# A reordered opening: conditioning loaded and turned alone, its Silu ahead of the rows' norm, a modulation chunk ahead of the turns

## The chip, the cores and the metric

The kernel runs on one core of a Trainium2 chip (trn2). The metric is the device time of one execution in microseconds. The same program is run several times and the median counts. Beside the times stands one profiled execution, whose span (first to last instruction) is a little different from the median; prices are read from it.

## What is computed

Two layers of a hybrid trunk over two tiles of 128 tokens (a context prompt and a latent sample), width 1024. Each layer has a mixer and a mixture of 32 experts. Every norm is modulated by a linear function of a conditioning vector, one for each tile:

```python
mod = jax.nn.silu(cvec) @ w_mod[l] + b_mod[l]
sh1, sc1, g1, sh2, sc2, g2 = jnp.split(mod[:, None, :], N_MOD, axis=-1)
h = rms_norm(x, norm_mix[l]) * (1.0 + sc1) + sh1
# layer 0: h -> differential attention and gated DeltaNet; layer 1: h -> gated spatial mixing
x = x + g1 * out
h = rms_norm(x, norm_ffn[l]) * (1.0 + sc2) + sh2
x = x + g2 * hier_moe(h, ...)
```

`cvec` is `c_ctx` for the context tile and `c` for the latent tile. All is float32. The weights of one layer's modulation are 1024 x 6144, and nearly all of the kernel's 288 MB read from HBM are weights.

## The kernel before

The program is written by hand, engine by engine, with semaphores. `P` is 128, `KT` is 8 (blocks of the width), `NB` is 2 (tiles). Activations are kept turned: `xT` and `hT` hold features on partitions and tokens in the free dimension.

**Weights.** SyncE's queue issues all weight loads in the order of a list, `loads`, written out by hand. A piece of 2 MB (a "chunk": 1024 rows by 512 columns) goes as two loads of 1 MB into one of four ring slots or six further slots, and its slot must have been freed (semaphore `used`, raised by TensorE's last matmul on the piece). The list begins with the modulation chunks (0,0) and (0,2), then the lower halves of two pieces of `w_in_even`, then chunks (0,1) and (0,3). Ahead of them the queue loads the identity and the ones, `const[:, 0:2P]` (line 802).

**ScalarE's queue** issues 12 loads before any arithmetic (lines 1585 to 1596): the rows of the two tiles (`xin`), the conditioning vectors `c_ctx` and `c` (16 rows of `vec1`), the constants up to `C_LEV` (which hold triangles, rotation tables, routing tables and, near the end, epsilon), and then bias, norm weights, convolution weights and two small vectors into `vec1` and `vec2`.

**The opening on TensorE** (lines 832 to 903), in order: wait for all ten small loads (`ld_vec`) and turn `vec1` and `vec2` into bank 0; wait for `xin` and the constants; turn the normalised rows `xn` of tile 0, then of tile 1, 8 blocks of 128x128 each (`rows_in`, line 842); clear bank 7 with a matmul of zeros; wait for `condT`; modulation chunks (0,0) and (0,2), 64 matmuls each (`mod_chunk`, line 861); turn the raw rows of tile 0; turn the modulation's result (`mod_turn`, line 870); and so on to the first projection (`first_rows`, line 908).

**The opening on VectorE** (lines 2014 to 2025): wait for the turned vectors and copy them to `cols` (bias, norm weights, conditioning and convolution taps, one column each); then wait for the scales and scale tile 0's rows into `xn`; then copy the turned rows out of PSUM.

**The opening on ScalarE** (lines 1640 to 1653): load the table of logarithm and exponential, wait for `xin` and the constants, two squares with a sum along the row, logarithm and exponential (`inv_root`), which give the scales `xsum`; scale tile 1's rows; load the Silu table; wait for `cols`, and take the Silu of the conditioning's 16 columns into `condT`.

Later, at line 1670, ScalarE's queue loads the rest of the constants, and behind it eleven small loads, with the gate weights `wab` first.

Of the kernel before, what the change touches and what calls it, by code (L numbers as in the profile page):

```python
# [24 lines left out]
P = 128  # L25
# [66 lines left out]
C_ID, C_ONE, C_TRI = 0, P, 2 * P  # L92
# [10 lines left out]
C_EPS = C_COL + 3  # L103
C_LEV = C_EPS + 2
# [8 lines left out]
V_COND = V_NMIX + DEPTH * KT  # L113
V_NFFN = V_COND + NB * KT
# [52 lines left out]
class Semaphores:  # L167
# [3 lines left out]
    def __init__(self, sem):  # L171
        self.a_ab = sem("a_ab")
# [37 lines left out]
        self.ld_attn = sem("ld_attn")  # L210
        self.ld_const = sem("ld_const")
# [19 lines left out]
        self.t_at = sem("t_at")  # L231
        self.t_cy = sem("t_cy")
# [34 lines left out]
        self.v_abx = sem("v_abx")  # L267
# [10 lines left out]
        self.v_gll = sem("v_gll")  # L278
# [40 lines left out]
def build(nc, I, O):  # L319
    ctx = ExitStack()  # L320
    with ctx:
# [43 lines left out]
        def part(at, shape):  # L365
            n = int(np.prod(shape))
            v = scratch[:, at:at + n]
            if len(shape) == 2:
                v = v.rearrange("p (a b) -> p a b", b=shape[1])
            elif len(shape) == 3:  # L370
                v = v.rearrange("p (a b c) -> p a b c", b=shape[1], c=shape[2])
            elif len(shape) == 4:
                v = v.rearrange("p (a b c d) -> p a b c d", b=shape[1], c=shape[2], d=shape[3])
            return v
# [17 lines left out]
        xin = part(2 * P, (NB, D))  # L392

# [266 lines left out]
        def _(sp):  # L660
# [141 lines left out]
            sp.dma_start(const[:, 0:2 * P], I["consts"][:, 0:2 * P]).then_inc(S.ld_vec, 16)  # L802
# [22 lines left out]
        def _(pe):  # L825
# [6 lines left out]
            pe.wait_ge(S.ld_vec, 16 * 10)  # L832
            nc.tensor.transpose(bank[0][:, 0:P], vec1[:, :], ident)
            nc.tensor.transpose(bank[0][:, P:P + 86], vec2[0:86, :], const[0:86, C_ID:C_ID + 86]).then_inc(S.t_x, 1)
            pe.wait_ge(S.ld_x, 32)
            pe.wait_ge(S.ld_const, 16)
# [8 lines left out]

            pe.wait_ge(S.v_xt, 1)
            rows_in(xn, 0, (1, 2))
            pe.wait_ge(S.a_xt, 1)
            rows_in(xn, 1, (3, 4))
# [47 lines left out]
            mod_chunk(0, 0)  # L897
            mod_chunk(0, 2)
# [88 lines left out]
            pe.wait_ge(S.v_ab, 1)  # L987
            for g in range(4):
                last = mm(bank[6][:, g * H:(g + 1) * H], tri[g % 2], gdec[:, g * H:(g + 1) * H], start=True, stop=True)
# [584 lines left out]
        def _(act):  # L1574
# [9 lines left out]

            act.dma_start(xin[:, 0, :], I["x_prompt"][0]).then_inc(S.ld_x, 16)
            act.dma_start(xin[:, 1, :], I["x_sample"][0]).then_inc(S.ld_x, 16)
            act.dma_start(vec1[112:120, :], I["c_ctx"].rearrange("(m p) -> m p", p=P)).then_inc(S.ld_vec, 16)
            act.dma_start(vec1[120:128, :], I["c"][0].rearrange("(m p) -> m p", p=P)).then_inc(S.ld_vec, 16)
            act.dma_start(const[:, 2 * P:C_LEV], I["consts"][:, 2 * P:C_LEV]).then_inc(S.ld_const, 16)
# [49 lines left out]

            roots()  # L1640
            act.wait_ge(S.ld_x, 32)
            act.wait_ge(S.ld_const, 16)
# [9 lines left out]
            act.wait_ge(S.v_cols, 1)  # L1652
            A(condT[:, :, :].rearrange("p t k -> p (t k)"), cols[:, V_COND:V_COND + NB * KT], ACT.Silu).then_inc(S.a_silu_c, 1)
# [16 lines left out]
            act.dma_start(const[:, C_LEV:NC_COLS], I["consts"][:, C_LEV:NC_COLS]).then_inc(S.ld_const, 16)  # L1670
# [76 lines left out]
            act.wait_ge(S.v_abx, 1)  # L1747
# [5 lines left out]
            A(t16a, t16a, ACT.Ln, bias=onec).then_inc(S.a_ab, 1)  # L1753
# [33 lines left out]
            act.wait_ge(S.v_gll, 1)  # L1787
# [191 lines left out]
        @block.gpsimd  # L1979
        def _(pool):  # L1980
            pool.memset(zeros[:, :], 0.0).then_inc(S.g_set, 1)

            pool.memset(raw[:, :, :, 0:2].rearrange("p c t n -> p (c t) n"), 0.0)
            pool.memset(raw[:, :, :, P + 2:P + 4].rearrange("p c t n -> p (c t) n"), 0.0).then_inc(S.g_set, 1)
            pool.wait_ge(S.ld_const, 32)
            for lev in range(1, NLEV + 1):
                for t in range(NB):
                    if lev == 1:
                        pool.wait_ge(S.v_att, 2 * t + 2)
                    else:  # L1990
                        pool.wait_ge(S.t_lx, 2 * lev - 3 + t)
                    nc.gpsimd.tensor_tensor(blk_B[t], blk_L[t], level(FIRST - 1 + lev), ALU.mult).then_inc(S.g_bm, 1)

            for t in range(NB):
                pool.wait_ge(S.a_y1, t + 1)
                pool.wait_ge(S.g_bm, 2 * NLEV)
                for d in range(2):
                    g, r = 2 * t + d, slice(d * HB, d * HB + HB)
                    nc.gpsimd.tensor_tensor(heads(g_V[g][r, :]), heads(y1s[t][r, :]),
                                            beta[r, g * H:(g + 1) * H].unsqueeze(2).to_broadcast([HB, H, P]), ALU.mult).then_inc(S.g_v1, 1)  # L2000
# [3 lines left out]
        def _(dve):  # L2004
# [123 lines left out]
            V.tensor_reduce(lame, lamq.rearrange("p (a n) -> p a n", a=2), AX.X, ALU.add).then_inc(S.v_abx, 1)  # L2128
            convolve(2)
            dve.wait_ge(S.a_ab, 1)  # L2130
# [10 lines left out]
            dve.wait_ge(S.ld_const, 32)  # L2141
# [56 lines left out]
            def delta_rows(t):  # L2198
# [27 lines left out]
                if t == 0:  # L2226
                    V.tensor_tensor(ekd, gll[:, 0:8], gcc[:, 0:8], ALU.subtract).then_inc(S.v_gll, 1)
# [448 lines left out]
```

## Time and profile before

| | before |
|---|---|
| median of 3 executions | 857.33 us |
| lowest to highest | 852.7 to 859.1 us |
| span of the profiled execution | 856.0 us |
| TensorE busy | 787.9 us, 92% |
| mean DMA throughput | 340 GB/s, 291.47 MB |
| mean granted TensorE clock | 0.971 |

The profiled execution lies 1.3 us under the median and well inside the spread of the three. All instants below are microseconds from the start of the span. TensorE's busy time includes waits inside its pipeline and is no measure of its peak.

### The profile page before, as it was taken

Reading aid. Unit: us, or ns where it says so; the run is one execution under the profiler, and the core shown is the slowest. Engines: PE = TensorE matmul, PEld = TensorE weight load, DVE = VectorE, ACT = ScalarE, POOL = GpSimd, SP = SyncE. Lnnn points to the kernel's source line nnn. Section 1 sums busy time; section 2 is a strip of 40 time slices with the busy share of each in tenths; the row PEclk is TensorE's granted clock in tenths of the full one; section 3 lists DMA queues with packets and bytes.
Section 4 is the critical chain, followed back from the end, with each engine's and each line's share of the span. In section 5 each row is a group of like instructions: output and inputs, shape, how many; then the busy total and the mean of one; then the engine's idle time right before and its main releaser. Section 6 shows DMA issues by size and latency. Waiting matters only on the chain.

```text
span 856.0 us, 15977 instructions
## 1 busy us (share of the span) xinstructions
PE 787.9 (92%) x6913; PEld 524.1 (61%) x6913; DVE 321.9 (38%) x687; ACT 166.7 (19%) x323; POOL 12.7 (1%) x17
## 2 busy tenths in 40 slices
PE   4999999998999999999787889989999999978797
PEld 3788577677898655565444344889865465534344
DVE  1154467653415434333413240241534433440224
ACT  3112321322204111111110141211311111110012
POOL 0000001020000000000000000000000000000000
PEclk9998999999999999999989999999999999997898
DMA  9999579496997799999999999994579999999991
GB/s 343 387 347 334 197 248 354 148 346 211 293 410 272 281 384 361 387 416 416 418 415 411 399 384 386 392 399 141 197 306 363 357 377 417 415 419 416 410 396 66
DMA packets 97879, 291.47 MB, mean 340 GB/s; under 512 B 11833, under 2 KB 14991, under 8 KB 87567
## 3 DMA queue, kind: packets, MB, share of 16 engines
q1 hardware_dynamic: 86960, 284.32, 86.5%
q10 hardware_dynamic: 10847, 6.11, 2.4%
q8 instruction: 56, 0.92, 0.4%
q14 instruction: 16, 0.13, 0.0%
HBM read 288.30 MB, written 2.10 MB: 339 GB/s over the span
## 4 chain that ended last, share of the span: by engine, by line
PE 72%; DMA 11%; SPq 8%; DVE 3%; ACT 2%; issue 2%; ACTq 1%; DVEq 0%
PE psum L1358 7%; PE psum L1265 7%; PE psum L1344 6%; PE psum L1334 6%; PE psum L908 6%; DMA scratch<-in_w_exp_up 6%; PE psum L1390 5%; PE psum L968 5%; SPq L745 5%; PE psum L861 4%; DMA ring<-in_w_exp_up 4%; PE psum L1401 3%; PE psum L1516 3%; PE psum L1529 3%; PE psum L1030 2%
## 5 line engine op out<-in xcount | busy, mean ns | idle before, releaser
L1344 PE MATMUL psum<-scratch,hT 128*32 128x512 f32 (+1 forms) x352 | 79.2, 666 | 17.6 <-DMA scratch<-in_w_exp_up 17.6
L1334 PE MATMUL psum<-scratch 128*128 128x128 f32 x704 | 82.4, 275 | 1.0 <-DVE scratch L2461 1.0
L1334 PEld LDWEIGHTS psum<-scratch 128*128 128x128 f32 x704 | 80.3, 192 | 1.3 <-issue 1.3
L1344 PE MATMUL psum<-ring,hT 128*32 128x512 f32 x320 | 60.1, 630 | 10.7 <-DMA scratch<-in_w_exp_up 10.7
L908 PE MATMUL psum<-hT,ring 128*128 128x256 f32 x256 | 57.8, 382 | 1.1 <-DVE hT L2052 0.7
L1401 PEld LDWEIGHTS psum<-const,scratch 128*128 128x128 bf16 x480 | 45.1, 97 | 21.4 <-issue 13.6
L1265 PE MATMUL psum<-hT,ring 128*128 128x128 f32 x512 | 58.0, 275 | 0.0
L1265 PEld LDWEIGHTS psum<-hT,ring 128*128 128x128 f32 x512 | 57.7, 192 | 0.5 <-issue 0.5
L1401 PE MATMUL psum<-const,scratch 128*128 128x256 bf16 x480 | 55.9, 272 | 1.5 <-DVE scratch L2477 1.5
L2470 DVE TENSOR_SCALAR hT<-psum,const 128x512 f32<-128x512 f32 x22 | 16.5, 751 | 106.3 <-PE psum L1390 93.6
L908 PEld LDWEIGHTS psum<-hT,ring 128*128 128x128 f32 x256 | 47.8, 190 | 9.6 <-DVE hT L2052 2.0
L1358 PE MATMUL psum<-scratch,hT 128*64 128x512 f32 (+1 forms) x256 | 50.0, 594 | 2.4 <-DMA ring<-in_w_exp_up 2.4
L1886 ACT ACTIVATE scratch<-psum 128x256 f32<-128x256 f32 x22 | 8.4, 383 | 221.3 <-PE psum L1344 133.6
L1390 PE MATMUL psum<-scratch,const 128*32 128x512 f32 (+2 forms) x336 | 50.9, 596 | 0.0
L1344 PEld LDWEIGHTS psum<-ring,hT 128*32 128x32 f32 x320 | 15.6, 115 | 53.4 <-issue 53.4
L1344 PEld LDWEIGHTS psum<-scratch,hT 128*32 128x32 f32 (+1 forms) x352 | 22.4, 128 | 39.7 <-issue 39.7
L861 PE MATMUL psum<-ring,condT 128*2 128x128 f32 x1344 | 43.4, 285 | 1.7 <-issue 1.0
L2481 DVE TENSOR_TENSOR scratch<-psum,scratch 128x256 f32<-128x256 f32 x22 | 9.3, 425 | 94.2 <-ACT scratch L1886 94.1
L968 PE MATMUL psum<-ring,hT 128*128 128x512 f32 x96 | 42.6, 597 | 0.0
L861 PEld LDWEIGHTS psum<-ring,condT 128*2 128x2 f32 x1344 | 34.6, 88 | 9.0 <-issue 4.7
L1358 PEld LDWEIGHTS psum<-scratch,hT 128*64 128x64 f32 (+1 forms) x256 | 15.3, 127 | 33.3 <-issue 33.2
L968 PEld LDWEIGHTS psum<-ring,hT 128*128 128x128 f32 x96 | 17.8, 190 | 20.8 <-issue 20.8
(328 smaller groups left out, 977.0 us busy)
## 6 DMA issues: line engine op xcount, KB each, us to landing
ring<-in_w_mod SPq DMA_DIRECT2D x42, 1024.0 KB, 9.5
scratch<-in_w_exp_down SPq DMA_DIRECT2D x36, 1024.0 KB, 18.1
scratch<-in_w_exp_gate SPq DMA_DIRECT2D x22, 1024.0 KB, 18.3
scratch<-in_w_exp_up SPq DMA_DIRECT2D x22, 1024.0 KB, 18.5
ring<-in_w_exp_gate SPq DMA_DIRECT2D x18, 1024.0 KB, 16.5
ring<-in_w_exp_up SPq DMA_DIRECT2D x18, 1024.0 KB, 18.4
scratch<-in_w_exp_gate SPq DMA_DIRECT2D x32, 512.0 KB, 13.3
scratch<-in_w_exp_up SPq DMA_DIRECT2D x32, 512.0 KB, 13.9
```

Of the source, the lines that this page charges most:

```text
L745: sp.dma_start(slot(s)[:, at:at + 1024], w[e][:, 1024 * kh:1024 * kh + 1024]).then_inc(full[s], 16)
L861: last = mm(bank[mbank[g]][32 * m:32 * m + NB, at:at + P], condT[:, :, k], w[:, k, m * P:(m + 1) * P], start=(k == 0), stop=(k == KT - 1))
L908: last = mm(out[:, c2 * T:(c2 + 1) * T], w[:, k, m * P:(m + 1) * P], hT[:, k, :, :], start=(k == 0 and k1 == KT), stop=(k == k1 - 1), skip ...
L968: last = mm(bank[b], hT[:, k, t, :], w[:, k, :], start=(k == 0), stop=(k == KT - 1))
L1265: last = mm(bank[2 * t + m // 4][:, (m % 4) * P:(m % 4 + 1) * P], w[m // 4][:, k, (m % 4) * P:(m % 4 + 1) * P], hT[:, k, t, :], start=(k = ...
L1334: last = mm(bank[b][:, k * P:(k + 1) * P], hrow[:, t, half * 4 + k, :], Pm[:, t, :], start=(t == 0), stop=(t == 1))
L1344: last = mm(bank[0][i * m:(i + 1) * m, :], xg[:, k, i * m:(i + 1) * m], w[e][:, k, :, :], start=(k == 0), stop=(k == KT - 1))
L1358: last = mm(bank[0][i * m:(i + 1) * m, :], xg[:, 4 * kh + k, i * m:(i + 1) * m], w[i // 2][:, i % 2, k, :, :], start=(kh == 0 and k == 0), ...
L1390: last = mm(bank[1 + half][i * m:(i + 1) * m, :], hidT[:, a, i * m:(i + 1) * m], slot(slots[e // 2])[:, base:base + 512], start=(a == 0), ...
L1401: last = mm(bank[4 + k // 2][:, (k % 2) * T:(k % 2 + 1) * T], y3[:, j, k, :], ohT, start=False, stop=True, skip_group_check=True)
L1516: last = mm(bank[4 + 2 * j + t], hT[:, k, t, :], w[:, k, :], start=(k == 0), stop=(k == KT - 1))
L1529: last = mm(bank[b][:, (m % 2) * T:(m % 2 + 1) * T], w[:, k, m * P:(m + 1) * P], hT[:, k, :, :], start=(k == 0), stop=(k == KT - 1))
```

## The change

- The conditioning vectors get a buffer of their own (`cond_rows`) and are the first two loads on ScalarE's queue, ahead of the rows. With the first load of constants they count on a new semaphore, `ld_cond`.
- Epsilon moves next to identity and ones, so that the first load on SyncE's queue brings it. The load of the other constants at the start is gone; they come with the later load, which is now `C_TRI` to the end.
- TensorE first turns the 16 conditioning rows alone into bank 5. The turns of `vec1` (now 112 rows) and `vec2` become a function, `vector_columns`, which is called behind modulation chunk (0,0). The row turns stand behind that, and chunk (0,2) behind them.
- ScalarE loads the Silu table first, takes the Silu of the conditioning straight from PSUM, and then loads the other table and goes on with the rows' squares.
- Three semaphores are merged into others (`a_ab` into `a_e1`, `v_abx` into `v_ab`, `v_gll` into `v_att`), and waits on the constants are adapted to one load.

```diff
-C_ID, C_ONE, C_TRI = 0, P, 2 * P
+C_ID, C_ONE, C_EPS = 0, P, 2 * P
+C_TRI = C_EPS + 2
...
-C_EPS = C_COL + 3
-C_LEV = C_EPS + 2
+C_LEV = C_COL + 3
...
-V_COND = V_NMIX + DEPTH * KT
-V_NFFN = V_COND + NB * KT
+V_NFFN = V_NMIX + DEPTH * KT
...
+        cond_rows = part(2 * P + NB * D, (P,))
...
-            sp.dma_start(const[:, 0:2 * P], I["consts"][:, 0:2 * P]).then_inc(S.ld_vec, 16)
+            sp.dma_start(const[:, 0:C_TRI], I["consts"][:, 0:C_TRI]).then_inc(S.ld_cond, 16)
...
-            pe.wait_ge(S.ld_vec, 16 * 10)
-            nc.tensor.transpose(bank[0][:, 0:P], vec1[:, :], ident)
-            nc.tensor.transpose(bank[0][:, P:P + 86], vec2[0:86, :], const[0:86, C_ID:C_ID + 86]).then_inc(S.t_x, 1)
-            pe.wait_ge(S.ld_x, 32)
-            pe.wait_ge(S.ld_const, 16)
+            pe.wait_ge(S.ld_cond, 16 * 3)
+            nc.tensor.transpose(bank[5][:, 0:NB * KT], cond_rows[0:NB * KT, :], const[0:NB * KT, C_ID:C_ID + NB * KT]).then_inc(S.t_cond, 1)
+
+            def vector_columns():
+
+                pe.wait_ge(S.ld_vec, 16 * 7)
+                nc.tensor.transpose(bank[0][:, 0:V_NFFN], vec1[0:V_NFFN, :], const[0:V_NFFN, C_ID:C_ID + V_NFFN])
+                nc.tensor.transpose(bank[0][:, V_NFFN:NV], vec2[0:86, :], const[0:86, C_ID:C_ID + 86]).then_inc(S.t_x, 1)
...
-            pe.wait_ge(S.v_xt, 1)
-            rows_in(xn, 0, (1, 2))
-            pe.wait_ge(S.a_xt, 1)
-            rows_in(xn, 1, (3, 4))
...
             mod_chunk(0, 0)
+            vector_columns()
+            pe.wait_ge(S.v_xt, 1)
+            rows_in(xn, 0, (1, 2))
+            pe.wait_ge(S.a_xt, 1)
+            rows_in(xn, 1, (3, 4))
             mod_chunk(0, 2)
             pe.wait_ge(S.a_xt, 3)
             rows_in(xin, 0, (4, 5))
...
             pe.wait_ge(S.v_ab, 1)
+            pe.wait_ge(S.ld_const, 16)
             for g in range(4):
...
+            act.dma_start(cond_rows[0:KT, :], I["c_ctx"].rearrange("(m p) -> m p", p=P)).then_inc(S.ld_cond, 16)
+            act.dma_start(cond_rows[KT:2 * KT, :], I["c"][0].rearrange("(m p) -> m p", p=P)).then_inc(S.ld_cond, 16)
             act.dma_start(xin[:, 0, :], I["x_prompt"][0]).then_inc(S.ld_x, 16)
             act.dma_start(xin[:, 1, :], I["x_sample"][0]).then_inc(S.ld_x, 16)
-            act.dma_start(vec1[112:120, :], I["c_ctx"].rearrange("(m p) -> m p", p=P)).then_inc(S.ld_vec, 16)
-            act.dma_start(vec1[120:128, :], I["c"][0].rearrange("(m p) -> m p", p=P)).then_inc(S.ld_vec, 16)
-            act.dma_start(const[:, 2 * P:C_LEV], I["consts"][:, 2 * P:C_LEV]).then_inc(S.ld_const, 16)
...
+            gates()
+            act.wait_ge(S.t_cond, 1)
+            A(condT[:, :, :].rearrange("p t k -> p (t k)"), bank[5][:, 0:NB * KT], ACT.Silu).then_inc(S.a_silu_c, 1)
             roots()
             act.wait_ge(S.ld_x, 32)
-            act.wait_ge(S.ld_const, 16)
+            act.wait_ge(S.ld_cond, 16 * 3)
             for t in range(NB):
...
             gates()
-            act.wait_ge(S.v_cols, 1)
-            A(condT[:, :, :].rearrange("p t k -> p (t k)"), cols[:, V_COND:V_COND + NB * KT], ACT.Silu).then_inc(S.a_silu_c, 1)
...
-            act.dma_start(const[:, C_LEV:NC_COLS], I["consts"][:, C_LEV:NC_COLS]).then_inc(S.ld_const, 16)
+            act.dma_start(const[:, C_TRI:NC_COLS], I["consts"][:, C_TRI:NC_COLS]).then_inc(S.ld_const, 16)
...
-            act.wait_ge(S.v_gll, 1)
+            act.wait_ge(S.v_att, 4)
             A(ekd, ekd, ACT.Exp).then_inc(S.a_kd, 1)
```

## Rows read from the trace of the kernel before

**Rows 1.** The page's engine table: busy us, share of the span, instructions.
```profile
PE 787.9 (92%) x6913; PEld 524.1 (61%) x6913; DVE 321.9 (38%) x687; ACT 166.7 (19%) x323; POOL 12.7 (1%) x17
```

**Rows 2.** Chain of waits in order of time, opening: start us, us, what.
```profile
1.17 0.46 ACTq L1586
...
2.64 0.37 ACTq L1589
...
5.63 5.88 DMA scratch<-in_subln
...
11.55 0.47 PE psum L833
...
12.21 0.38 DVE cols L2015
12.59 0.67 DVE scratch L2017
...
13.40 3.65 PE psum L842 x16
...
17.59 4.08 PE psum L861 x128
21.66 1.02 PE psum L842 x8
```

**Rows 3.** Chain of waits, 44 to 69 us.
```profile
44.57 14.07 PE psum L908 x64
...
59.06 9.27 DMA ring<-in_w_mod
```

**Rows 4.** Stretches: length, busy PE, PEld, DVE, ACT, POOL, PEclk, DMA share, GB/s.
```profile
10.00:12.00 2.00, 0.45 (x2) 0.29 (x2) 0.00 (x0) 1.94 (x5) 0.00 (x0) 1.00 1.06 379
...
54.00:56.00 2.00, 2.00 (x11) 1.77 (x10) 2.00 (x6) 0.00 (x0) 0.00 (x0) 1.00 0.56 177
```

**Rows 5.** DMA issues: KB each, us from issue to landing.
```profile
scratch<-in_x_sample ACTq DMA_DIRECT2D x1, 512.0 KB, 6.4
...
const<-in_consts ACTq DMA_DIRECT2D x1, 308.5 KB, 6.7
...
const<-in_consts ACTq DMA_DIRECT2D x1, 416.0 KB, 6.9
```

**Rows 6.** Timeline of ScalarE, opening: start us, us, engine, line, operation.
```profile
5.98 1.28 ACT L1579 ACT_TABLE_LOAD   x1 [5.98 <-issue]
...
9.45 1.06 ACT L1646 ACTIVATE scratch<-scratch 128x1024 f32<-128x1024 f32 x1 [2.19 <-DMA const<-in_consts]
...
12.13 0.20 ACT L1603 ACTIVATE small<-small 128x2 f32<-128x2 f32 x1
```

**Rows 7.** View of line L699, one load: the second half of chunk (0,0).
```profile
L699 SPq DMA_DIRECT2D ring<-in_w_mod x1: 500/500/500, 1.6 to 1.6; - x1
DMA to landing us min/median/max: 11.2/11.2/11.2
```

**Rows 8.** TensorE: ns min/median/max, first to last start us; stretch as rows 4; timeline.
```profile
L842 PE MATMUL psum<-const,scratch x7: 421/421/421, 14.7 to 16.0; 128*128 128x128 f32 x7
...
L861 PE MATMUL psum<-ring,condT x12: 273/372/418, 18.1 to 18.6; 128*2 128x128 f32 x12
...
80.00:86.80 6.80, 6.80 (x76) 5.21 (x77) 4.99 (x18) 0.82 (x5) 0.00 (x0) 0.50 0.77 269
...
32.79 1.93 PE L861 MATMUL psum<-scratch,condT 128*2 128x128 f32 x64
...
81.53 3.60 PE L861 MATMUL psum<-ring,condT 128*2 128x128 f32 x64
```

**Rows 9.** Timeline and one line's view: first uses of what lands later.
```profile
77.24 4.35 PE L952 MATMUL psum<-wab,hT 128*128 128x16 f32 x32
...
99.35 1.22 DVE L2146 SCALAR_TENSOR_TENSOR scratch<-scratch 128x1024 f32<-128x1024 f32 x1
...
L1788 ACT ACTIVATE small<-small x1: 200/200/200, 166.7 to 166.7; 128x8 f32<-128x8 f32 x1
```

## What the change will do: the prediction

> **What bounds the kernel now.** I read the page's engine table first: over the profiled span (856.0 us, table of times) TensorE (PE) is busy 787.9 us, VectorE 321.9, ScalarE 166.7 [rows 1]. So the kernel advances with TensorE and the weight transfers that feed it. The edit is all in the first 23 us, so the chain of waits of the opening comes next [rows 2]. TensorE does nothing until the last small vector has landed at 11.51. It turns the vectors (11.55 to 12.21, 0.66), VectorE copies the columns (0.38) and scales the first tile's rows (0.67, from 12.59), TensorE turns 16 blocks of rows (from 13.40, 3.65), clears a bank (17.05 to 17.59, 0.54) and does two modulation chunks, 128 matmuls, in 4.08. At 21.66 it goes on to the next turns, `mod_turn(M_LO)` and the first projection. I take this instant, "the end of chunk (0,2)", as the yardstick: everything behind it is unchanged in order.
>
> Whether a shift of that instant reaches the end is seen further down the chain [rows 3]. From 44.57 TensorE works unbroken to 58.64. Then the weight queue, which waited for a slot to be freed by that work, issues a load that lands 9.27 us later, and TensorE waits for it until 68.37. Each load on this stretch starts when TensorE frees its slot, so a shift of TensorE shifts the load. The DMA engines have room there: between 54 and 56 us their busy share was 0.56, against 1.06 between 10 and 12 [rows 4]. So I let the shift pass to the end whole, in both directions; where it did not, the rival "absorbed" below stands.
>
> **What goes from the front of the chain.** The old first wait (11.51) is gone as a release of the conditioning: the two 4 KB vectors are now first on ScalarE's queue, and identity, ones and epsilon come in one load on SyncE's queue at 0.72. Their landing has no row. From below they need at least their issue (nothing, counted from the issue), from above 512 KB of x_sample on the same queue took 6.4 us [rows 5]. I take some 3 us from their issues, as they are small and first; even if they landed at 11 nothing would change, since the chunk's weights are later (next part). The small turn, the zero matmul (0.54 in the chain) and the Silu (0.21 us of ScalarE) then lie in time in which TensorE was idle. ScalarE pays one more table load, 1.28 us [rows 6]. Its first table load began at 5.98, behind 12 issues of 0.4 to 0.5 us each; one of these, that of the constants, is gone. It used to start the squares only at 9.45, on the constants' landing. Now it runs: issues to 5.98 - 5.98/12 = 5.5, 5.6 taken, Silu's table to 6.9, Silu to 7.1, the other table to 8.4. x_sample landed at 1.17 + 6.4 = 7.6 [rows 2, 5], and both x loads are issued two issues later, about 1 us, so at 8.6 at worst. From squares to the scales takes 9.45 to 12.33, 2.9 us [rows 6], so they are there by 11.5. By the next part they are wanted at 16.5, so the extra table load and the later x cost nothing unless they slip by five more microseconds.
>
> **What sets the new chain: the weights of chunk (0,0).** In the old order its landing was hidden. Its second half was issued at 1.6 and took 11.2 us, so 12.8 [rows 7]. The diff takes the 308.5 KB load of constants out of the early traffic. It had landed at 2.64 + 6.7 = 9.3 [rows 2, 5], ahead of that half, so its bytes come off whole: 0.316 MB at 379 GB/s [rows 4] is 0.8 us. I take 12.0. The bound above is 12.8 (no byte argument). Chunk (0,2) is the next 2.1 MB of the queue, 5.5 us at that rate: 17.5.
>
> Behind this wait, in TensorE's own order, now stand the vectors' turns, and behind them on VectorE the copy `cols`, and behind that, in VectorE's order, the scaling of tile 0's rows. The rows' scales are ready at 11.5, but VectorE meets the column copy first in its program and waits there. So the chain is: 12.0, chunk (0,0), vector turns 0.66, then from the column copy to the first row turn (12.21 to 13.40) 1.19 us, idle for TensorE, 16 row turns, chunk (0,2).
>
> **TensorE's clock decides the prices.** The 16 row turns of 13.40 follow each other every 228 ns, the 8 of 21.66 every 128 [rows 2]; one of the former takes 421 ns, and the chunk's matmul goes from 418 to 273 ns between 18.1 and 18.6 [rows 8]. In the stretch 80.0 to 86.8, where the granted clock is 0.50 (1.2 GHz), the 64 matmuls of a chunk took 3.60 us, against 1.93 at 32.79, at the granted 1.00 (2.4 GHz) [rows 8]. The view of the granted clock shows 1.00 for 0 to 18.5 too, but the durations say the half level. So the 16 row turns ran at half speed (3.65 us, where 8 at full clock took 1.02), and the clock was full from about 18.5, 5.1 us after the unbroken work had begun at 13.40. The edit moves a chunk of 64 matmuls into the slow time: 3.5 us from its start to the next work where the old place cost under 2.
>
> The sum, with the old distance of 5.1 us from the start of the work to the full clock taken over (12.0 + 5.1 = 17.1, an estimate): 12.0 + 3.5 + 0.66 + 1.19 = 17.35, then 16 turns at full clock 2.05, then the chunk 1.9: 21.3. Before: 21.66. The gain is 0.3 to 0.4 us. Bare counting of what left the chain would have promised 0.54 + 2.04 = 2.6. The Trainium skill ("TensorE: Matmul & The Clock Gate", part 1) says that the default state is throttled and activity releases the throttle; by that rule the earlier work also brings the full clock earlier, which is the case "clock early" below, with its own price. The same page of the Trainium skill ("Architectural detail", part 1) calls VectorE's queue strictly first in, first out. That speaks against this edit, since the scaling then cannot overtake the column copy; the trace agrees, with scales ready at 12.13 + 0.20 = 12.33 [rows 6] and the scaling on the chain only from 12.59, where the copy ends [rows 2]. If it could overtake, the row turns could follow the vectors' turns at 16.15 and the sum would be 20.1.
>
> **The rest of the diff.** The later load of constants grows from 416 to 724.5 KB and is still one issue at 42.8. The small one took 6.9 us [rows 5]; scaled by bytes, 12 us, it lands near 55. The first instruction behind a wait for it is VectorE's L2146 at 99.35; the gate weights queued behind it on ScalarE's queue are read at 77.24 [rows 9]. At least 19 us lie before each of them: nothing. If the cover were gone it would cost what the bytes cost, 0.8 us; the total of bytes is the same. Three semaphores are merged. `v_att` 4 in place of `v_gll` comes later on VectorE, but ScalarE reaches that exponential (L1788) only at 166.7, behind `first_inverse(0)`, which itself waits for work that VectorE does after the last `v_att` [rows 9]: nothing. Shorter turns and a copy of 198 instead of 214 columns: under 0.05 us.
>
> Sum: 856.0 - 0.3 = 855.7 for a profiled execution; against the median of 857.33, which lies 1.3 above it, 857.0.
>
> **Rivals.**
> Clock early: the clock is full before the chunk's end or from its start. From the start: 12.0 + 1.9 + 0.3 + 1.2 + 2.05 + 1.9 = 19.4, 2.2 us less than 21.66; near its end, 0.8 less. For it: TensorE starts 1.4 us earlier than 13.4 and does denser work than the broken start at 11.55. Against it: it is a cold start in both. Time 855.1 to 856.5.
> Clock late, the one on the other side: the idle 1.2 us between the vectors' turns and the row turns breaks the work, and the clock rises only 5.1 us after the row turns start, at 22.5. Then 17.4 + 3.65 = 21.05, 1.45 us of the chunk at half speed (0.41 of it), the rest 1.1: 23.6, 1.9 us later than before. It decides as soon as the clock is still at half when the first row is turned. For it: the old start too had a break (12.2 to 13.4) and the rise came only 5.1 us after the break. Time 859.2.
> Absorbed: the opening ends earlier but the transfers after it don't, so 857.3. For it: TensorE waited 0.8 us for a load at 68.4. Against it: that load starts with a slot that TensorE frees.
> Half-clock stretches fall elsewhere: there is one at 80 to 86.8 us, and every other stretch after it moves with the work. One more or less of that length costs 6.8 x 0.5 = 3.4 us; the three runs of before spread from 852.7 to 859.1, which such stretches may explain. Two or three of one sign would be needed to pass 1%.
>
> **Chances.** Forecast (-0.3) 0.40; clock early 0.22; clock late 0.25; absorbed 0.06; moved stretches that carry it beyond 1% 0.07, split 0.03 faster and 0.04 slower. The first four lie between 855.1 and 859.2. To them comes the spread of a median of few runs: the fastest run of before, 852.7, and the slowest, 859.1, which with the late clock's 1.9 is 861.0. So 852.5 to 861.0. About 1% is what a measurement of this kernel can tell from no change: faster 0.03, same 0.93, slower 0.04.
>
> **What would show it.** In the changed profile: the conditioning's turn near 4 to 5 us and its Silu by 7.2; ScalarE's squares starting at 8 to 9 and the scales by 11.6; TensorE idle until the landing of chunk (0,0) at about 12.0, 64 matmuls in about 3.5 us; the row scaling on VectorE right behind the column copy, near 16.6, and not at 11.5; the first row turn at 17.4; the end of chunk (0,2) at 21.3, and 228 or 128 ns from one row turn to the next to tell the clock cases. At 58 and 68 us the same shift should be seen. I am wrong if chunk (0,0) lands well before 11 (the order of the two queues matters more than bytes), if the scaling does not wait for the columns, or if a shift at 22 us is not there at 68 us.

## The result, and the profile after

The changed kernel takes 858.93 us in the median of 22 executions (854.95 to 864.2), the kernel before 856.06 us beside it, in as many (852.7 to 860.47). The ratio is 1.0027, 95% interval [1.0014, 1.004]: slower by 2.3 us (the two medians lie 2.9 apart). That is less than 1%, so inside what the prediction called the same, but it is a loss where a gain of 0.3 us was forecast. The changed kernel was timed against the one before twice more, on other occasions, with 12 executions of it each (runs `c1_changed_again` and `f2_changed_third`): 0.9998 [0.997, 1.0025] and 1.0009 [0.9983, 1.0034]. Weighting the three by the inverse square of their half-widths gives 1.0019 with a half-width of 0.0011, so some 1.7 us. Executions more than 1.5% above the fastest of their kernel are left out of all ratios here (one of `f1_cols_first_again` at 1021.46 us, two of `c4_warm12` at 867.89 and 868.09), though not out of the medians.

The engine table of the changed kernel's first profile has nearly the numbers of [rows 1]; this one execution (853.9 us of span) is even shorter than the one profiled before (856.0), though the medians stand the other way. A single profile can't carry a difference of 2 us here.

```profile
span 853.9 us, 15978 instructions
...
PE 787.4 (92%) x6914; PEld 523.3 (61%) x6914; DVE 321.7 (38%) x687; ACT 167.9 (20%) x324; POOL 12.7 (1%) x17
```

The chain of waits of that profile (start us, us, what) answers to [rows 2] and [rows 3]. Line 858 is the chunk's matmul, 844 the row turns, 837 the vectors' turns, 910 the projection:

```profile
1.65 10.60 DMA ring<-in_w_mod
...
12.38 3.48 PE psum L858 x64
15.87 0.25 PE psum L837
...
16.23 0.37 DVE cols L2018
16.59 0.67 DVE scratch L2020
...
17.31 1.97 PE psum L844 x16
19.27 1.86 PE psum L858 x64
21.13 1.02 PE psum L844 x8
...
58.53 9.76 DMA ring<-in_w_mod
...
68.33 1.93 PE psum L858 x64
```

The opening is the predicted chain almost to the tenth: the wait for the weights of chunk (0,0), the chunk at half clock in 3.5 us, the vectors' turns, the column copy and, behind it, the row scaling, the first row turn at 17.31 (forecast 17.4), the end of chunk (0,2) at 21.13 (forecast 21.3, before 21.66). The 0.53 us won are gone at 68.33, where the chain of before also stood (68.37). So this execution explains no loss. A second and a third profile of the same kernel (chain of waits again, first `c1_changed_again`) look otherwise:

```profile
12.30 3.59 PE psum L858 x64
...
17.53 3.50 PE psum L844 x16
21.04 1.86 PE psum L858 x64
22.90 1.03 PE psum L844 x8
...
60.31 9.86 DMA ring<-in_w_mod
```

and now `f2_changed_third`:

```profile
12.29 3.60 PE psum L858 x64
...
17.53 3.68 PE psum L844 x16
21.21 1.96 PE psum L858 x64
23.16 1.02 PE psum L844 x8
...
60.57 9.95 DMA ring<-in_w_mod
...
70.56 1.47 PE psum L858 x45
```

Up to 17.5 us all three agree within 0.25 us. Then the same 16 row turns take 1.97 us in the first and 3.50 and 3.68 in the others: full clock against half. Chunk (0,2) ends at 22.9 and 23.2, the delay reaches 70.2 and 70.6 where chunk (0,5) starts. This is the rival "clock late" (forecast 23.6). In this text "late branch" stands for these two openings.

What the opening does and what the whole execution takes are not tied closely. The spans of the three changed profiles are 853.9, 854.6 and 862.6 us, those of the three profiles of before 856.0, 853.9 and 857.1. The second changed profile is a late branch and still ends among the shortest. The chains show what the opening costs up to 70 us; that this makes the difference of the medians is an inference, supported by the timings below and not proved by any one profile.

### The profile page after: what moved, and what is told of

The parts are those of the page before. It is cut to its first block, busy times and chain, and to the rows that moved or that the text cites. A ratio compares the mean times of both kernels' runs of the same rounds, so it can differ in the third digit from the quotient of the medians.

```text
span 853.9 us, 15978 instructions
## 1 busy us (share of the span) xinstructions
PE 787.4 (92%) x6914; PEld 523.3 (61%) x6914; DVE 321.7 (38%) x687; ACT 167.9 (20%) x324; POOL 12.7 (1%) x17
## 4 chain that ended last, share of the span: by engine, by line
PE 74%; DMA 11%; SPq 6%; DVE 3%; ACT 2%; issue 2%; ACTq 1%; DVEq 0%
PE psum L1347 8%; PE psum L1361 7%; PE psum L1337 7%; PE psum L1268 7%; PE psum L910 6%; PE psum L1393 6%; DMA scratch<-in_w_exp_up 5%; PE psum L970 5%; PE psum L858 4%; PE psum L1404 4%; DMA ring<-in_w_exp_up 4%; PE psum L1519 3%; PE psum L1532 3%; SPq L744 3%; DMA ring<-in_w_mod 2%; PE psum L1033 2%
## 5 line engine op out<-in xcount | busy, mean ns | idle before, releaser
L1347 PE MATMUL psum<-ring,hT 128*32 128x512 f32 x320 | 60.1, 630 | 10.7 <-DMA scratch<-in_w_exp_up 10.7
## 6 DMA issues: line engine op xcount, KB each, us to landing
scratch<-in_w_exp_down SPq DMA_DIRECT2D x36, 1024.0 KB, 17.5
```

Of the source, the lines that this page charges most:

```text
L1347: last = mm(bank[0][i * m:(i + 1) * m, :], xg[:, k, i * m:(i + 1) * m], w[e][:, k, :, :], start=(k == 0), stop=(k == KT - 1))
```

## The experiments

In all of them "before" is the kernel before, run beside. The experiments came in five groups, each on one chip; ratios within a group share their "before". Two theories are tried. The theory "clock": the idle 1.2 us between the vectors' turns and the row turns lets the full clock come late in part of the executions. The theory "constants": the grown later load of constants holds up the weights issued at 51 us. These are two loads of 1 MB of `w_in_even`, on the same queue ahead of those for chunk (0,5); their landing below is that of the first.

**One part undone or moved.** `e1_const_back` restores the early load of the constants:

```diff
+            act.dma_start(const[:, C_TRI:C_LEV], I["consts"][:, C_TRI:C_LEV]).then_inc(S.ld_const, 16)
             act.dma_start(vec1[0:DEPTH * MT, :], ...)
...
-            act.dma_start(const[:, C_TRI:NC_COLS], ...)
+            act.dma_start(const[:, C_LEV:NC_COLS], ...)
```

> The changed kernel, with the constants loaded in two parts again as before (C_TRI to C_LEV early, behind the x loads; the rest at the later place). Theory 'constants': the later load, grown by 0.3 MB, holds up the weights queued at 51 us by up to 0.8 us, so this kernel is 0.6 to 0.8 us faster than the changed one, ratio to before 1.0017 to 1.002, and in its trace w_in_even's first half issued near 51 lands before 59.7 instead of 60.16. Theory 'clock': the loss is the row turns and chunk (0,2) done at half clock in some executions; then nothing changes, ratio 1.0027, the landing may move but the time does not.

Measured: 857.67 us, ratio 1.0005 [0.9991, 1.002]. Chunk (0,0) starts at 13.13 instead of 12.3 (the 0.8 us of the early bytes, as argued in the prediction), the row turns take 1.97, chunk (0,5) starts at 68.33. Taken alone, this interval holds the 1.0017 to 1.002 that "constants" asked for and not the 1.0027 of "clock"; against the pooled 1.0019 of the changed kernel it separates nothing. In the trace the weights land at 60.1, not before 59.7.

`e2_cols_first` puts the vectors' turns ahead of the chunk:

```diff
-            mod_chunk(0, 0)
             vector_columns()
+            mod_chunk(0, 0)
             pe.wait_ge(S.v_xt, 1)
             rows_in(xn, 0, (1, 2))
```

> The changed kernel, with the vectors' turns ahead of chunk (0,0) instead of behind it, so that the column copy and the row scaling run under the chunk and TensorE's work is unbroken from its start near 12.3. Theory 'clock' (the idle 1.2 us behind the chunk delays the full clock and the loss comes from that): row turns begin at about 15.9, chunk (0,2) ends at 19.6 to 20.9 in every execution, the ratio to before falls to 0.999 to 1.001. Theory 'constants': the opening does not matter since the load at 68 us lands at the same time anyway; ratio stays at 1.002 to 1.003.

Measured: 855.89 us (853.52 to 857.31), ratio 0.9987 [0.9972, 1.0002]. The chain of its opening:

```profile
13.15 3.53 PE psum L858 x64
16.67 2.12 PE psum L844 x16
18.79 1.86 PE psum L858 x64
20.66 1.02 PE psum L844 x8
```

The row turns follow the chunk without a gap, and the end of chunk (0,2) is at 20.66, 1.0 us ahead of before, as the theory "clock" expects. The interval of the ratio lies wholly under that of the changed kernel's first timing.

`e3_warm` fills the idle time ahead of the chunk with matmuls:

```diff
+            for _ in range(18):
+                mm(bank[7][:, 0:2 * P], ident, const[:, 0:2 * P], start=True, stop=True)
             def vector_columns():
```

> The changed kernel with 18 added matmuls of the identity on the constants (128x256, their result is thrown away) in TensorE's idle time between the conditioning's turn at 4.7 us and chunk (0,0) at 12.3. Theory 'clock': the chunk runs at full clock (1.9 us instead of 3.5), the row turns start near 15.6, chunk (0,2) ends near 19.6, and the time falls to that of before or under it, ratio 0.998 to 1.0005. Theory 'constants' or any other cause behind 40 us: the opening is earlier by 1.5 us in the trace, the time is not, ratio 1.002 to 1.003.

Measured: 857.44 us, ratio 1.0004 [0.9987, 1.0022]. The filling ran until 14.7 and so past the landing: chunk (0,0) started at 15.0, at full clock (1.86 us). Chunk (0,2) ended at 22.15, so the run did not give the earlier opening that was wanted. The end of chunk (0,2) is later than in any profile of before, but chunk (0,5) starts at 68.50, level with before, and so is the time.

`e4_chunk_back` moves chunk (0,0) behind the row turns:

```diff
-            mod_chunk(0, 0)
             vector_columns()
...
             rows_in(xn, 1, (3, 4))
+            mod_chunk(0, 0)
             mod_chunk(0, 2)
```

> The changed kernel with chunk (0,0) back behind the row turns, next to chunk (0,2); all else as changed. Row turns begin near 14.4 (scales at 13.5), chunk (0,2) ends near 22 us, about 0.4 later than before and 0.9 later than in the changed kernel's profile. Theory 'clock': unbroken work as in before, so the loss against before falls to 0.3 to 0.6 us, ratio 1.0005. Theory 'constants': ratio 1.002 to 1.003, as nothing behind 40 us is altered.

Measured: 858.28 us (854.13 to 863.4), ratio 1.0006 [0.9985, 1.0026]. Row turns from 14.37, end of chunk (0,2) at 22.66. The mean is as "clock" has it; the interval also holds 1.002, so it does not exclude the rival.

**The changed kernel again, both causes together, a measured delay.** `c1_changed_again` is the changed kernel:

> The changed kernel as it is, as the control on the same chip as the three beside it. Both theories: ratio to before 1.0014 to 1.004, as measured first. Its one profile shows either the plateau (first half of the weights issued at 51 us lands near 60.1, chunk (0,5) starts at 68.3) or, by the theory 'step', a late branch (landing at 62 or later, chunk (0,5) from 70 or later).

Measured: 857.05 us, ratio 0.9998 [0.997, 1.0025]. The mean lies under the 1.0014 to 1.004 expected. Its profile is the late branch shown above. The weights issued at 53.0 landed at 62.0, as the theory "step" of the expectation has it.

`c2_cols_first_const_back` has the edits of `e2_cols_first` and `e1_const_back` together:

> The changed kernel with the vectors' turns ahead of chunk (0,0) and the constants in two loads as before. If the two causes add (idle 1.2 us in the opening; grown load of constants at 42 us), this is the fastest of the four: ratio 0.996 to 0.999. If only the opening counts, it equals the kernel with the vectors' turns first alone, 0.9987. If the later load does not matter at all and the early one delays chunk (0,0) by 0.8 us, it is slower than that, 0.999 to 1.000.

Measured: 858.34 us, ratio 1.0016 [0.9994, 1.0039]. This is a miss: it was to be 1.000 at most, and it is slower than `e2_cols_first` was. Its profile says why for that execution: the last small vector landed only at 13.9 (it comes last on ScalarE's queue, now behind the constants), and since the vectors' turns go first, chunk (0,0) waited for them until 14.6. The row turns took 2.78 us and chunk (0,2) ended at 22.75. With the vectors first, the early constants are in the way.

`c3_before_delay2` adds a delay to the kernel before:

```diff
             for b in (1, 2, 3):
                 mm(bank[b], zeros[:, 0:128], zeros[:, 0:512], start=True, stop=True)
+            for _ in range(10):
+                mm(bank[1], zeros[:, 0:128], zeros[:, 0:512], start=True, stop=True)
```

> The kernel before with ten added matmuls of zeros (about 2.1 us) on TensorE ahead of the first projection, near 24 us; nothing else. This measures what a late opening costs. Theory 'step': beyond about 52.5 us the weights issued there land not later by the shift but by a jump (62 or later instead of 60.2), chunk (0,5) waits, the granted clock falls to half behind the wait, and the kernel loses more than was added: 4 to 5 us, ratio 1.0045 to 1.006. Theory 'passes whole': 2.1 us, ratio 1.0025. Theory 'absorbed': ratio 1.000 to 1.001.

Measured: 860.29 us, ratio 1.004 [1.0018, 1.0063], 3.4 us. In its profile the end of chunk (0,2) is at 21.37 and chunk (0,3) ends 1.45 us later than that implies; the rest of the 2.1 us fell into TensorE's old wait for the modulated rows. Chunk (0,5) starts at 69.06, only 0.7 us behind the mean of before (68.38). The ratio says at least 1.5 us at the end (1.8 thousandths of 857), so the lateness isn't absorbed; but the interval holds the 2.1 us of "passes whole" as well as the 4 to 5 us of "step". The jump that "step" wanted is not there in this kernel, which has the constants in two loads: weights issued at 52.9 land 6.0 us later, at 58.9.

`c4_warm12` is `e3_warm` with 12 matmuls instead of 18:

> The changed kernel with 12 added matmuls of the identity (each recorded as two) in the idle time of the opening instead of 18, which had run past the landing of chunk (0,0). The chunk should start at its landing near 12.3 at full clock, 1.9 us; chunk (0,2) ends at 19.5 to 20. Theory 'clock': the loss against before is gone, ratio 0.998 to 1.000. Theory 'constants': ratio 1.002 or more.

Measured: 862.87 us (854.34 to 868.09), ratio 1.0047 [1.0014, 1.0079]: a clear miss, and one against the theory "clock" as the whole account, since this kernel's clock is full before the first chunk. Its profile (855.2 us of span) has the opening that was wanted, the earliest of all:

```profile
12.36 1.93 PE psum L861 x64
...
15.73 1.97 PE psum L847 x16
17.70 1.86 PE psum L861 x64
19.55 1.02 PE psum L847 x8
...
56.95 10.03 DMA ring<-in_w_mod
67.03 1.93 PE psum L861 x64
```

Of the 2.1 us won at 22 us against before, 1.3 are left at 67 us. Yet 8 of its 12 executions took 862 us or more.

**Side by side, and more profiles of before.** `f1_cols_first_again` and `f2_changed_third` ran on one chip:

> The changed kernel with the vectors' turns ahead of chunk (0,0), once more, beside the changed kernel on the same chip. Theory 'clock' (the idle 1.2 us between the vectors' turns and the row turns lets the full clock come late in a part of the executions): faster than the changed kernel, by 1 to 3 us, ratio to before 0.998 to 1.000, and a narrow spread (4 us where the changed kernel spreads over 8). Rival 'chance' (the two openings cost the same and the first measurements differed by noise): the two ratios agree within 0.001.

> The changed kernel, control of the one beside it. Ratio to before 1.001 to 1.003 by the theory 'clock', and the profile shows the clock full near 15.6 (chunk (0,2) ends at 21.1) or near 20.7 (ends at 22.9). By 'chance' ratio 1.000 to 1.001.

Measured: 855.89 us, 0.998 [0.9954, 1.0007], and 857.79 us, 1.0009 [0.9983, 1.0034]. The counted executions of the first spread over 6.9 us (852.3 to 859.19), not over the 4 us expected. In the profiles the first ended chunk (0,2) at 20.16 and started chunk (0,5) at 66.95; the second is the late branch above. The order is as "clock" has it, 1.9 us between the medians, though the two intervals overlap. Pooled over two timings of this order and three of the changed kernel, the ratios are 0.9985 with a half-width of 0.0013 and 1.0019 with 0.0011; these do not overlap. That the place of the vectors' turns matters, by some 3 us, is shown by this.

> The kernel before, unchanged, for a second profile: how far its own opening varies. Theory 'clock': its work is unbroken from 13.4 us, so chunk (0,2) ends within 21.0 to 22.3 whatever the moment of the full clock; never near 23. The half-clock stretch at 80 us may be absent, 3.4 or 6.8 us long.

> The kernel before, a third profile, same expectation: chunk (0,2) ends within 21.0 to 22.3, chunk (0,5) starts at 68.3 to 68.6.

Measured: 855.68 and 858.87 us, one execution each. Chain of waits of `g1_before_look`:

```profile
13.47 3.65 PE psum L842 x16
...
17.43 3.61 PE psum L861 x128
21.04 1.02 PE psum L842 x8
```

and of `g2_before_look`:

```profile
13.58 3.65 PE psum L842 x16
...
17.76 4.10 PE psum L861 x128
21.86 1.03 PE psum L842 x8
```

The row turns of before are at half clock in all three profiles (3.65 us), and the two chunks behind them mostly or wholly at full clock, so the ends of chunk (0,2) lie between 21.04 and 21.86. Chunk (0,5) starts at 68.26 to 68.50.

**What the long executions of the warmed kernel lose.** Two more profiles:

> The changed kernel with 12 warming matmuls, a look for a slow execution (862 us and over). If the earlier end of the opening makes TensorE wait longer for chunk (0,5) near 65 us, the granted clock falls to half there or at 80 us for 6.8 us or more, and chunk-by-chunk the delay against the other profiles shows up between 65 and 110 us. If the clock falls again inside the opening (during the wait for the weights or the 1.2 us of VectorE), chunk (0,2) ends at 21 or later instead of 19.6.

> The same kernel again, same expectation; a fast execution (854 to 858) ends chunk (0,2) near 19.6 and starts chunk (0,5) near 67.0.

Measured: 863.77 and 854.09 us, a long one and a short one. Both openings are early (chunk (0,2) ends at 20.54 and 20.29, chunk (0,5) starts at 67.84 and 67.14). So nearly all of the 10 us between them arises elsewhere. The views by stretch (length, busy PE, PEld, DVE, ACT, POOL, granted clock, DMA share, GB/s), the long one first:

```profile
80.00:86.80 6.80, 6.80 (x82) 5.45 (x82) 6.24 (x21) 0.82 (x5) 0.00 (x0) 0.75 0.88 297
...
226.00:356.00 130.00, 125.81 (x1062) 91.61 (x1055) 47.18 (x130) 25.43 (x56) 0.00 (x0) 0.97 0.88 329
```

```profile
80.00:86.80 6.80, 6.80 (x136) 5.74 (x127) 6.66 (x22) 2.42 (x6) 0.00 (x0) 1.00 1.05 390
...
226.00:356.00 130.00, 127.18 (x1034) 88.50 (x1035) 49.36 (x131) 24.35 (x54) 0.00 (x0) 0.99 0.89 347
```

At 80 us the long one has half of the stretch at half clock, the short one none of it; between 226 and 356 us it has a lower mean clock and moves 329 GB/s instead of 347, which over 130 us is 2.3 MB, or 7 us at that rate (an estimate). Of the expected places the stretch at 80 us takes part, with under 2 us (0.25 of 6.8); the opening and the wait at 65 us don't. Why the warmed kernel meets this more often than the others is open.

**The constants, with the lateness held equal.** `h3_const_late_delay2` is the kernel before with the changed kernel's loads of constants and the delay of `c3_before_delay2`:

> The kernel before with the constants loaded as in the changed one (epsilon with the first load, all others in one load at 43 us) and with ten added matmuls of zeros, 2.1 us, ahead of the first projection. Theory 'grown load': the weights issued near 53 us land at 61.5 to 62 and chunk (0,5) starts at 70.0 to 70.5. Theory 'late issue alone': they land near 59 as with the delay alone, and chunk (0,5) starts at 69.1.

Measured: 863.03 us, one execution. Its ScalarE waited for the last small load until 10.43, so the row turns began 0.9 us later than before (14.34) and chunk (0,2) ended at 22.82; it issued the weights at 54.3 and not at 52.9. They landed at 61.5, chunk (0,5) started at 70.44. With this second difference it can't be compared with its partner. The next two were meant to settle it: both have the 12 warming matmuls, so no clock case, and a delay that puts chunk (0,4) at 59.6 and 58.9; apart from the length of the delay they differ in the constants' loads alone.

```diff
+            for _ in range(12):
+                mm(bank[7][:, 0:2 * P], ident, const[:, 0:2 * P], start=True, stop=True)
...
+            for _ in range(14):
+                mm(bank[1], zeros[:, 0:128], zeros[:, 0:512], start=True, stop=True)
```

(In `i2_fixed_const_early` the second loop has 11, and the constants are loaded as in `e1_const_back`.)

> The changed kernel with 12 warming matmuls, so that the clock is full from the first chunk in every execution, and 14 added matmuls of zeros (2.9 us) ahead of the first projection, so that chunk (0,4) starts at 59.5 to 60.3 as in the changed kernel's late executions. Constants as in the changed kernel. Theory 'grown load': the weights issued near 53 us land near 62 and chunk (0,5) starts 10.3 to 10.5 us after chunk (0,4), at 70.2 or later. Rival 'clock alone': it starts 9.3 to 9.5 us after it.

> The same with the constants in two loads as before, and 11 added matmuls (the chunk's weights land some 0.7 us later), so that chunk (0,4) starts at about the same time. Theory 'grown load': the weights land near 59 to 60 and chunk (0,5) starts 9.3 to 9.6 us after chunk (0,4). Rival: no difference to its partner.

Measured: 861.17 and 854.66 us, one execution each, which in a kernel with this spread decide nothing. The views of the weights' line, one load each (issue, us to landing), `i1_fixed_const_late`:

```profile
L698 SPq DMA_DIRECT2D ring<-in_w_in_even x1: 368/368/368, 52.8 to 52.8; - x1
DMA to landing us min/median/max: 6.6/6.6/6.6
```

and the changed kernel's `c1_changed_again`, nearly the same issue:

```profile
L698 SPq DMA_DIRECT2D ring<-in_w_in_even x1: 368/368/368, 53.0 to 53.0; - x1
DMA to landing us min/median/max: 9.0/9.0/9.0
```

With the grown load the weights land after 6.6 us in `i1_fixed_const_late`, and with two loads after 7.0 in `i2_fixed_const_early`; chunk (0,5) starts 9.2 and 9.6 us behind chunk (0,4). In this pair the grown load costs nothing. But the pair does not stand for the kernels without a delay. There, at nearly the same issue, three profiles with the grown load landed late (`c1_changed_again`, `f2_changed_third` and `e4_chunk_back`, at 61.9 to 62.0), and `c2_cols_first_const_back`, with two loads, landed at 59.2:

```profile
L698 SPq DMA_DIRECT2D ring<-in_w_in_even x1: 368/368/368, 52.8 to 52.8; - x1
DMA to landing us min/median/max: 6.4/6.4/6.4
```

In the late ones the DMA engines stood almost still for a while. The view by stretch, first `c1_changed_again`, then `c2_cols_first_const_back`, then `i1_fixed_const_late`:

```profile
55.00:56.00 1.00, 1.00 (x6) 0.90 (x5) 1.00 (x4) 0.00 (x0) 0.00 (x0) 1.00 0.02 1
...
55.00:56.00 1.00, 1.00 (x6) 0.89 (x5) 1.00 (x4) 0.00 (x0) 0.00 (x0) 1.00 0.96 252
...
55.00:56.00 1.00, 1.00 (x6) 0.90 (x5) 1.00 (x4) 0.00 (x0) 0.00 (x0) 1.00 0.87 166
```

Of the twenty profiles four have this gap (DMA share 0.02 to 0.09 between 55 and 56 us): these three and `h3_const_late_delay2`. All four have the grown load and issue the weights at 52.7 or later. `i1_fixed_const_late` has both and no gap; none of the seven profiles with two loads has one, though two of them issue the weights as late as 52.8 and 52.9. So a late opening together with the grown load may cost more than either alone. The theory "constants" in this form is not excluded; the runs do not decide it, and what makes the gap is open.

**A version from the findings.** `h4_cols_first_const_last` has `e2_cols_first`'s order and the constants behind the small loads:

> The changed kernel with the vectors' turns ahead of chunk (0,0) and with the load of constants behind the ten small loads on ScalarE's queue instead of ahead of them. If the grown load holds up what is queued behind it, the small loads end earlier (before 57), the weights issued near 50.5 land before 58.5, and the kernel is at or under the 0.998 to 0.9987 of the version without this, down to 0.997. If the many small packets themselves hold up the weights, nothing changes: 0.998 to 0.9987.

Measured: 856.96 us, ratio 0.9996 [0.9978, 1.0015]. The small loads end at 55.0, before 57 as expected, yet the weights issued at 51.6 land only at 59.5, 8.0 us later, where `e2_cols_first` had 8.1: no gain from the constants' place at this issue time. The profile has row turns of 2.87 us and the end of chunk (0,2) at 21.47, late for this order.

## Why the prediction was wrong

**The chain.** Right, by row: what the new chain is, that VectorE's copy stands ahead of the scaling, chunk (0,0)'s landing (12.0 forecast, 12.25 measured; 13.0 with the early constants back), the conditioning's turn at 4.7, its 3.5 us at half clock, the first row turn (17.4; 17.3 and 17.5). Wrong without effect: x_sample landed at 10.6, not by 8.6 (probably since the weights' queue was served ahead of it; no run shows this), so the squares began at 10.65 instead of 8 to 9 and the scales were there at 13.5 instead of 11.6. They were wanted at 16.6, so the slack of five microseconds shrank to three. The grown load of constants took 7.7 us and not the 12 scaled by bytes, so it landed at 50.0 and not near 55.

**The step that failed** is the one where the old distance of 5.1 us between the start of the work and the full clock was taken over, which put it at 17.1. From this the sum took one value, 2.05 us, for the 16 row turns. In the four profiles with this opening the 16 row turns took 1.97 us (the first profile and `e1_const_back`) or 3.50 and 3.68. The clock is full before the break of 1.2 us, or it comes only some 3 to 4 us behind it; in these four nothing lies between. The prediction had both as rivals, at 0.22 and 0.25, and put the mass on a value inside the idle time. The sum of the forecast case (21.3) and the first profile (21.13) agree because a clock that is full anywhere before the first row turn gives the same row turns; it is the mean over the executions that the sum missed. Where the work is unbroken, durations between occur: 1.91, 2.12, 2.78 and 2.87 us for the row turns of the four kernels with the vectors first, one profile each. Before the change the break was there too (12.2 to 13.4), but only 0.7 us of work lay ahead of it; the row turns behind it ran at half clock in all three profiles, the chunks behind them mostly at full clock, and the spread was 0.8 us. The edit put 3.9 us of work ahead of the break, and in two of four profiles that work brought no full clock behind it. Why one or the other happens, no run shows.

**The price.** Mean end of chunk (0,2): before 21.5 (three profiles), changed 22.4 (three). Mean start of chunk (0,5): 68.4 and 69.7. That is 1.3 us, where the pooled ratio says 1.7, with 0.9 to either side. These are few profiles; the size agrees, and the measured 2.3 us of the first timing lies near the upper end of it. It is agreement in size and no proof: `c4_warm12` takes this price away (chunk (0,5) at 67.03) and is slower all the same.

**Passing to the end.** The prediction let a shift pass whole in both directions. The runs show no such rule in either direction. Of gains, the 0.5 us of the first profile had become 0.04 at 68 us and the 2.1 us of `c4_warm12` 1.3, but `f1_cols_first_again` kept 1.4 of 1.5. Of delays, the two late branches grew, from 1.2 and 1.5 us to 1.8 and 2.2, while `c2_cols_first_const_back` went from 1.1 to 0.8 and the delay of `c3_before_delay2` shrank to 0.7 by 69 us (though its time grew by at least 1.5). The delays that grew are three (with `e4_chunk_back`), and all three have the gap in the DMA traffic at 55 us. So a second step is in doubt, the term that the prediction put at nothing for the grown load of constants: it looked at who needs the constants and not at the weights issued after them. That the load costs something in executions that are late already is argued from the profiles; no timing isolates it. Absorption on its own, to which I gave 0.06, took part of most shifts.

**The rest.** Nothing in the runs speaks against the merged semaphores being free. That the half-clock stretch at 80 us comes and goes was forecast and seen: the three profiles of before have 6.8 us, none and 6.8 us of it, all three of the changed kernel half of that:

```profile
80.00:86.80 6.80, 6.80 (x84) 5.39 (x84) 5.53 (x20) 0.82 (x5) 0.00 (x0) 0.75 0.85 296
```

This is the changed kernel's first profile, granted clock 0.75, against 0.50 in [rows 8]. It is worth 1.7 us there (3.4 us at half, an estimate), but it does not explain why this execution ends earlier than that of before, since it has other half-clock stretches that the latter lacks (mean granted clock 0.969 against 0.971). Between 213.6 and 217.0, the profile of before first, then the changed kernel's:

```profile
213.60:217.00 3.40, 2.02 (x36) 1.95 (x38) 3.37 (x6) 0.60 (x1) 0.20 (x1) 1.00 0.50 200
...
213.60:217.00 3.40, 3.40 (x44) 3.40 (x41) 2.42 (x5) 0.60 (x1) 1.38 (x2) 0.50 0.26 26
```

**A better version.** The variant that comes out best is the changed kernel with the vectors' turns ahead of chunk (0,0). Its two timings, 0.9987 [0.9972, 1.0002] and 0.998 [0.9954, 1.0007], weighted as above give 0.9985 with a half-width of 0.0013: about 1.3 us under the kernel before. It is faster than the changed kernel beyond the intervals; against the kernel before its lead is barely clear of them, and `h4_cols_first_const_last`, with the same opening, came out at 0.9996 [0.9978, 1.0015].

## What to carry to other kernels

Here a chunk moved into the cold start of TensorE won at most 0.5 us in the opening, and the break right behind it went with openings 1.2 to 1.5 us later than before in two of four profiles: look whether the work ahead of the full clock stays in one piece, and fill the break by putting the releasing work (here 0.6 us of turns) ahead of the moved one. Where a clock or a queue has two outcomes, forecast both and their mean, not the value between them. When a load grows, look not only at who needs it but also at the loads issued after it, in a late execution as well as in an early one. A single profile of a kernel whose executions spread over 1% proves the chain, not the sign of a change of 0.3%.

## What the hardware showed that was not expected

- A float32 matmul (not a turn) stands in the trace as two records: the 12 added matmuls of `h1_warm12_look` appear as 24, in 7.3 us together. So a chunk is 32 matmuls, not 64 as the prediction says; its prices are per chunk and are not touched.
- Behind 18 such matmuls in the idle time (`e3_warm`), and behind 12 (`c4_warm12`), the chunk takes 1.86 and 1.93 us instead of 3.5: the clock was full by then.
- Two openings that are early by the same 1 to 2 us gave 854 and 864 us, with the larger part of the difference between 226 and 356 us (329 against 347 GB/s). An earlier start is no guarantee of an earlier end here, and what joins them was not found.
- With the constants in one grown load and the weights issued at 52.7 us or later, the share of the DMA engines fell to 0.02 to 0.09 between 55 and 56 us in four of five profiles; there the first half of the weights took 7.1 to 9.2 us to land. With the constants in two loads and the weights issued as late, it took 6.0 and 6.4.
